# One decoder pass on one core: narrower masked products, a reordered triangular inverse, paired output-projection products, and the dense FFN's norm applied at gating

## Chip, cores and metric

One NeuronCore of a Trainium2 chip runs the whole kernel in one launch. The metric is the device time of the launch in microseconds (us); the profile's times count from the first instruction.

## What is computed

Two layers over 256 tokens of width 1024, all in float32. Each layer: `x = x + mixers(rms_norm(x) @ w_in) @ w_out`, then `x = x + ffn(rms_norm(x))`, where

```python
y = x * rsqrt(mean(x * x, axis=-1) + eps);  return y * w      # rms_norm
(silu(h @ w1) * (h @ w3)) @ w2                                # swiglu
```

The mixers are four groups of 256 columns: y_a (an RWKV-7 recurrence), y_b (dilated attention), y_c (MLA attention, whose latents c_q and c_kv are normalised first) and y_d (HGRN2, a gated linear recurrence). Layer 0 has a dense FFN of 2816 hidden columns; layer 1 routes each token to 2 of 8 experts of 3584 hidden columns. A last rms_norm gives the output.

## The kernel before

Everything is kept feature-major: 128 partitions hold features, 256 tokens lie along the free dimension; `xT` holds x and `hT` the normed x (later the mixers' output `yT`) as 8 tiles of 128x256. A large product is made in three: weight and activation are each split in a rounded high part (ACT copies to `mh`/`oh`/`wh`, `xh`, `gh`) and a low part (DVE subtracts: `ml`/`ol`/`wl`, `xl`, `gl`), and TensorE adds high x high, high x low, low x high in PSUM. Products of the mixers' small matrices are plain float32, which TensorE does as two instructions each. The engines' programs are straight lists written by hand (`block.tensor`, `block.scalar`, `block.vector`, `block.gpsimd`, `block.sync`); each engine works through its own list in order, and semaphores tie them. `spin(b, n)` (line 463) issues n products whose result nobody reads.

**HGRN2 scores** (lines 1294 to 1306). Levels 0 to 7; for a level e the queries and keys are scaled on POOL (lines 1153 to 1180), PE makes 8 products of 64x128 by 64x128 per level, and DVE copies under a mask (`hgrn_mask`, line 1994) into `hs`. For e >= 1 the mask has ones only in the later half of each block of 2^e columns. The levels stand between the last column units of `w_in` (units 9 to 12).

**The triangular inverse** (lines 1504 to 1547). RWKV's chunk form needs the inverse of 8 triangular 128x128 matrices. It is built in levels l = 1 to 6. A level is: 16 products `mtd x xin` (PE), a copy to `pid` (ACT, line 1824), products giving `xin` and `xit` updates (PE), subtractions (DVE, lines 2116 to 2132). The two 64-row halves of a matrix are separate until level 6, which joins them. `beside(l, half)` (line 1486) puts attention work between: MLA queries (`mla_q`) in level 1, their rotary partner in 2 and 3, `mla_k` in 4, `mla_v`, `mla_kr` in 5, and dilated attention. The DVE part of that work is `side_step(l)` (line 2081): reciprocal of the HGRN norm in 1, rotary for queries in 2 and 3, y_d in 4, rotary key in 5. Before the levels, DVE normalises the MLA latents (lines 2071 to 2077), and `mla_q(0)` waits for them (`lat_ready`).

**Solve** (line 1566). With the inverse, four heads are solved per chunk: for each head one product over 64 rows (`xi0`) and one over 128 rows (`xit`), each 64 outputs wide.

**Output projection** (lines 665 to 696). `w_out` is four units of 256 columns; unit u is summed in bank 2 + u. Its eight row tiles are taken in two halves: part 0 is y_b and y_d (k = 2, 3, 6, 7), part 1 is y_a and y_c (k = 0, 1, 4, 5). `pe_out_half(q)`, q = 0 to 7, makes 24 products of 256 columns. q = 0 to 3 stand amid the last attention work; q = 4 to 7 follow `attend_out(1)`, which turns y_c, and each waits for a weight half that is split into one of two buffers.

**After it** (lines 1633 to 1644, 1871 to 1888, 2198 to 2212). DVE adds bank 2 + u to `xT`, ACT squares, PE sums the squares (`norm_part`), ACT takes the root, DVE the reciprocal and the eight products into `hT`. In layer 0 `hT` is then split into `xh`, `xl`, and only then the dense FFN can begin. On DVE the first weight split of the FFN (`up(0, 0)`) stands before the last addition to `xT`:

```python
                    if u == NO - 1:
                        up(0, 0)
                    dve.wait_ge(sem("out_used"), 2 * NO * layer + NO + u + 1)
                    tt_(flat(xT[:, 2 * u:2 * u + 2]), ..., bank[2 + u][:], ALU.add, "xT_ready")
```

**The dense FFN** (lines 440 to 461, 557 to 586). Eleven pairs of 2x128 hidden columns. For a pair, PE does `up` in two parts (48 products each, banks 0, 1 or 6, 7 in turn) and `down` of the pair before it (48 products into banks 2 to 5, cleared at first by `zero_acc`). ACT takes silu of one half of a bank, DVE multiplies with the other (`dve_gate`, line 542), ACT and DVE split the result. Weights come as 1 MB stages through a ring of 7 slots that SyncE fills; slots 4 to 6 may be filled once `out_used` says that the first q of part 1 is done (lines 1054 to 1063). The MoE FFN has the same structure with jobs of 128 tokens; it starts with routing in layer 1.

## Time and profile before

| | us |
|---|---|
| median of 3 runs | 1687.99 (1687.73 to 1689.75) |
| the profiled execution | 1691.8 |
| its span, first to last instruction | 1690.2 |
| mean granted TensorE clock | 0.983 |
| mixers of layer 0, about | 0 to 230 |
| its projection's end, norm, dense FFN | 230 to 454 |
| mixers of layer 1, about | 454 to 670 |
| its projection's end, norm, routing | 670 to 715 |
| MoE FFN and the end | 715 to 1690 |

How to read it: PE is TensorE's matmuls, PEld its weight loads, DVE VectorE, ACT ScalarE, POOL GpSimd. The chain of waits is followed back from the last instruction, so a stretch of it says what set the time there. A PEclk of 1.00 is 2.4 GHz, 0.50 is 1.2 GHz; values between are means over a stretch that has both.

### The profile page before, as it was taken

What the parts mean: (1) busy time and instruction counts of PE and PEld (TensorE: products, weight loads), DVE (VectorE), ACT (ScalarE), POOL (GpSimd) and SP (SyncE); (2) the same over time, 40 slices, a digit from 0 to 9 for tenths busy, and PEclk for the clock granted to TensorE, in tenths of its full rate; (3) what the DMA queues carried; (4) which work ended last, traced back from release to release, by engine and by line L of the source; (5) the groups of instructions that cost most, each with busy time, mean ns of one, the idle gap of its engine ahead of it and who ended that gap; (6) DMA issues with size and microseconds to landing.
All of it is one profiled execution on the core that took longest, in us unless ns stands there. A gap on an engine that the chain in (4) does not pass through costs nothing.

```text
span 1690.2 us, 27508 instructions
## 1 busy us (share of the span) xinstructions
PE 1606.6 (95%) x10176; PEld 1368.0 (81%) x10176; DVE 1305.3 (77%) x1212; ACT 1041.2 (62%) x1032; POOL 133.6 (8%) x150
## 2 busy tenths in 40 slices
PE   7988989999898898899999999999999999999997
PEld 7876779999897777778888888888888888888776
DVE  4886555454557774688898888888889888888997
ACT  4634354433444344477777777777777777777675
POOL 1151000000003310100000000000000000000620
PEclk9998999999999999999999999999999999999999
DMA  7429044543242200789999999999999999999993
GB/s 249 163 80 405 31 174 179 193 175 124 75 156 91 76 2 7 297 319 373 363 397 368 369 395 373 379 383 373 382 375 363 396 368 373 391 373 366 396 355 119
DMA packets 68269, 457.51 MB, mean 271 GB/s; under 512 B 7296, under 2 KB 8480, under 8 KB 16752
## 3 DMA queue, kind: packets, MB, share of 16 engines
q1 hardware_dynamic: 59984, 425.80, 65.7%
q0 software_dynamic: 8080, 30.84, 4.7%
q8 instruction: 40, 0.66, 0.2%
q14 instruction: 21, 0.17, 0.0%
q10 hardware_dynamic: 144, 0.05, 0.0%
HBM read 433.07 MB, written 23.59 MB: 270 GB/s over the span
## 4 chain that ended last, share of the span: by engine, by line
PE 78%; DVE 11%; issue 5%; ACT 5%; DMA 0%; DVEq 0%; SPq 0%; ACTq 0%
PE bank L402 32%; PE bank L427 16%; PE bank L405 8%; PE bank L1203 7%; PE bank L660 6%; PE bank L431 4%; DVE wl L482 2%; ACT wh L478 1%; PE bank L415 1%; PE bank L692 1%; DVE ml L647 1%; DVE hT L1920 1%; PE bank L1551 1%; ACT mh L641 1%; ACT wide L1660 1%
## 5 line engine op out<-in xcount | busy, mean ns | idle before, releaser
L482 DVE TENSOR_TENSOR wl<-ring,wh 128x2048 fp32r<-128x2048 f32 x369 | 854.7, 2319 | 179.2 <-ACT wh L478 176.0
L478 ACT ACTIVATE wh<-ring 128x2048 fp32r<-128x2048 f32 x369 | 705.6, 1914 | 119.2 <-PE bank L427 47.7
L402 PE MATMUL bank<-wh,xh 128*128 128x512 f32 x896 | 359.6, 401 | 5.0 <-DVE wl L482 3.1
L402 PE MATMUL bank<-wh,xl 128*128 128x512 f32 x896 | 350.6, 391 | 0.0
L402 PE MATMUL bank<-wl,xh 128*128 128x512 f32 x896 | 349.2, 390 | 0.0
L402 PEld LDWEIGHTS bank<-wh,xh 128*128 128x128 f32 x896 | 168.2, 188 | 38.3 <-DVE wl L482 4.0
L402 PEld LDWEIGHTS bank<-wh,xl 128*128 128x128 f32 x896 | 168.1, 188 | 37.1
L402 PEld LDWEIGHTS bank<-wl,xh 128*128 128x128 f32 x896 | 168.7, 188 | 32.4
L427 PE MATMUL bank<-wh,gh 128*128 128x512 f32 x448 | 175.4, 392 | 6.4 <-DVE gl L555 6.4
L427 PE MATMUL bank<-wl,gh 128*128 128x512 f32 x448 | 174.4, 389 | 0.0
L427 PE MATMUL bank<-wh,gl 128*128 128x512 f32 x448 | 174.4, 389 | 0.0
L504 ACT ACTIVATE silu<-bank,const 128x256 f32<-128x256 f32 x134 | 62.3, 473 | 113.4 <-PE bank L402 72.4
L641 ACT ACTIVATE mh<-ring 128x1024 fp32r<-128x1024 f32 (+1 forms) x52 | 53.0, 1025 | 101.5 <-PE bank L660 101.2
L660 PE MATMUL bank<-xh,mh 128*128 128x256 f32 x336 | 99.9, 297 | 14.0 <-DVE xl L611 7.2
L517 ACT ACTIVATE gh<-bank 128x256 fp32r<-128x256 f32 x112 | 42.9, 383 | 112.7 <-PE bank L415 112.7
L647 DVE TENSOR_TENSOR ml<-ring,mh 128x1024 fp32r<-128x1024 f32 (+1 forms) x52 | 62.2, 1204 | 56.2 <-ACT mh L641 55.5
L427 PEld LDWEIGHTS bank<-wh,gh 128*128 128x128 f32 x448 | 84.1, 188 | 26.3 <-DVE gl L555 6.3
L405 PE MATMUL bank<-xh,wh 128*128 128x256 f32 x352 | 101.0, 287 | 3.4 <-DVE xl L611 3.4
L405 PE MATMUL bank<-xh,wl 128*128 128x256 f32 x352 | 100.7, 286 | 0.0
L405 PE MATMUL bank<-xl,wh 128*128 128x256 f32 x352 | 100.7, 286 | 0.0
L427 PEld LDWEIGHTS bank<-wh,gl 128*128 128x128 f32 x448 | 84.1, 188 | 17.6
L427 PEld LDWEIGHTS bank<-wl,gh 128*128 128x128 f32 x448 | 84.1, 188 | 17.1
(329 smaller groups left out, 2461.7 us busy)
## 6 DMA issues: line engine op xcount, KB each, us to landing
ring<-in_moe_w SPq DMA_DIRECT2D x336, 1024.0 KB, 6.3
ring<-in_ffn_w SPq DMA_DIRECT2D x33, 1024.0 KB, 4.8
ring<-in_w_in SPq DMA_DIRECT2D x24, 1024.0 KB, 5.0
ring<-in_w_out SPq DMA_DIRECT2D x8, 1024.0 KB, 4.8
job_x<-xrow POOLq DMA_DIRECT2D x1, 8192.0 KB, 27.4
job_y<-xrow POOLq DMA_DIRECT2D x1, 8192.0 KB, 46.8
xrow<-job_x POOLq DMA_DIRECT2D x7, 512.0 KB, 9.8
job_y<-yj POOLq DMA_DIRECT2D x7, 512.0 KB, 6.2
```

The lines of the kernel that those rows point to most:

```text
L402: ins = nc.tensor.matmul(up_bank(run, par, 0)[:], x[:, 0:C], w[b][:, k], **kw)
L405: ins = nc.tensor.matmul(up_bank(run, par, item)[:, kind * T:(kind + 1) * T], w[b][:, k, at:at + P], x, **kw)
L427: ins = nc.tensor.matmul(bank[2 + o][:], g[:, a, 0:C], w[b][:, a, o * 512:(o + 1) * 512], start=first and a == 0 and g is gh and b == 0, s ...
L431: ins = nc.tensor.matmul(bank[2 + o // 2][:, o % 2 * T:(o % 2 + 1) * T], w[b][:, a, o * P:(o + 1) * P], g[:, a], start=False, stop=False, ...
L478: nc.scalar.activation(wh[:, buf], flat_slot(slot), ACT.Copy).then_inc(sem("w_high"), 1)
L482: nc.vector.tensor_tensor(wl[:, buf], flat_slot(run.place(i)[0]), wh[:, buf].bitcast(F32), ALU.subtract).then_inc(sem("w_split"), 1)
L504: nc.scalar.activation(silu[:, item], up_bank(run, par, item)[:, 0:T], ACT.Silu, bias=cst("zero")).then_inc(sem("silu_done"), 1)
L517: nc.scalar.activation(o, i, ACT.Copy).then_inc(sem("g_high"), 1)
L641: nc.scalar.activation(mh[:, part, :, 0:n], unit_weights(u)[:, 4 * part:4 * part + 4, 0:n], ACT.Copy).then_inc(sem("unit_high"), 1)
L647: nc.vector.tensor_tensor(ml[:, part, :, 0:n], unit_weights(u)[:, 4 * part:4 * part + 4, 0:n], mh[:, part, :, 0:n].bitcast(F32), ALU.subtr ...
L660: ins = nc.tensor.matmul(o[:, c * T:(c + 1) * T], l, r, start=part == c == k == n == 0, stop=part == 1 and k == 3 and n == 2, skip_group_c ...
L1203: ins = nc.tensor.matmul(o, l, r, start=start, stop=stop)
```

## The change

1. HGRN2 levels e >= 1: PE and DVE treat only the later half of each block (64 columns per head instead of 128).
2. The inverse is kept as full 128x128 matrices (`xft`; POOL clears one quarter), and the solve is two products over all 128 rows per head.
3. The MLA latents' normalisation goes from before the levels into level 1, behind its updates, and the MLA steps on PE, ACT and DVE go one level later (`mla_kr` goes ahead of `mla_v`, y_d to level 6).
4. Ahead of the solve, `r_tokens(0)` and `attend_scores(4)` no longer wait for the inverse, and two of three spins go.
5. Part 1 of the output projection is taken as four pairs of units: q = 4, 5 with y_a's rows (k = 0, 1), ahead of and behind `attend_out(1)`, q = 6, 7 with y_c's (k = 4, 5). The three spins behind `attend_out(1)` go. Splits and additions are reordered to match; `up(0, 0)` on DVE now stands behind all additions.
6. Layer 0 only: `xh`, `xl` are the split of x times the norm's weight. The FFN's first products start on them; squares and sum are made meanwhile. The factor per token (`rstd[:, 1]`) comes at gating: DVE multiplies both halves of each bank by it (`dve_scale`), silu then works on that. `zero_acc` is replaced by start flags and a first step outside the loop.

The diff, cut to its core:

```diff
+        xft = proj[:, 4:8].rearrange("p a (b c) -> p (a b) c", c=P)
...
-            with pe.Fori(0, n // 2) as i:
-                step(2 * i + 1, 1)
+            step(1, 1, True)
+            with pe.Fori(0, (n - 1) // 2) as i:
                 step(2 * i + 2, 0)
-            if n % 2:
-                step(n, 1)
+                step(2 * i + 3, 1)
+            if n % 2 == 0:
+                step(n, 0)
...
+        def dve_scale(dve, run, m, par):
+            for item in range(run.parts):
+                dve.wait_ge(sem("stage_used"), run.up(m, 1)[0] + 1)
+                wait(dve, "g_split", run.before_pairs + m)
+                b = up_bank(run, par, item)
+                nc.vector.tensor_tensor(silu[:, item], b[:, 0:T], rstd[:, 1], ALU.mult)
+                nc.vector.tensor_tensor(gate[:, item], b[:, T:2 * T], rstd[:, 1], ALU.mult).then_inc(sem("scaled"), 1)
...
             for m in range(1, run.pairs - 1):
                 dve_gated_low(dve, run, m - 1)
                 up(m + 1, 0)
+                if not run.moe:
+                    dve_scale(dve, run, m, m % 2)
+                    up(m + 1, 1)
                 dve_gate(dve, run, m, m % 2)
-                up(m + 1, 1)
+                if run.moe:
+                    up(m + 1, 1)
                 down(m)
...
-        def pe_ffn_dense(pe):
-            zero_acc((2, 3, 4, 5))
-            for part in range(2):
-                pe.wait_ge(sem("x_split"), x_before(0, 2) + part + 1)
-                pe_up(pe, dense, 0, 0, part)
+        def pe_ffn_dense(pe, norm):
+            pe.wait_ge(sem("x_split"), x_before(0, 2) + 1)
+            pe_up(pe, dense, 0, 0, 0)
+            norm(1)
+            pe.wait_ge(sem("x_split"), x_before(0, 2) + 2)
+            pe_up(pe, dense, 0, 0, 1)
+            pe.wait_ge(sem("std_ready"), 2)
             pe_steps(pe, dense)
...
+                settle(nc.gpsimd.memset(xft[H:P, :, 0:H], 0.0))
...
-                            mm(bank[6 + half][:, m * P:(m + 1) * P], src, qry, sig=...)
+                                o = bank[6 + half][:, m * P // 2:(m + 1) * P // 2]
+                                qry = later(hq[lo:hi, (e - 1) % 2, s], e)
+                            mm(o, src, qry, sig=...)
...
-                    if (l, half) in ((1, 0), (1, 1)):
+                    if l == 2:
                         mla_q(half)
-                    if (l, half) in ((2, 1), (3, 0)):
-                        mla_partner(l - 2)
-                    if (l, half) in ((4, 0), (4, 1)):
+                    if (l, half) in ((3, 1), (4, 0)):
+                        mla_partner(l - 3)
+                    if l == 5:
                         mla_k(half)
                     if (l, half) == (5, 0):
+                        mla_kr()
+                    if (l, half) == (6, 0):
                         mla_v()
-                    if (l, half) == (5, 1):
-                        mla_kr()
...
-                        mm(o[0:H], xi0[0:H, m], rsol[0:H, h])
-                        mm(o[H:P], xit[:, m], rsol[:, h], sig=...)
+                        for q in (0, H):
+                            mm(bank[6][q:q + H, h * HD:(h + 1) * HD], xft[:, mat(h, c), q:q + H], rsol[:, h], sig=...)
...
+                r_tokens(0)
+                attend_scores(4)
                 spin(4, 1)
                 pe.wait_ge(sem("xit_ready"), nth(2 * LEVELS, 2 * LEVELS - 1))
-                r_tokens(0)
-                attend_scores(4)
-                spin(4, 2)
                 solve(0)
...
                 spin(6, 3)
+                pe.wait_ge(sem("ya_low"), nth(1))
+                pe_out_pair(pe, layer, NO, False)
                 attend_out(1)
-                spin(6, 3)
-                for u in range(NO):
-                    pe_out_half(pe, layer, NO + u)
-                    if u:
-                        norm_part(2 * layer + 1, u - 1)
+                pe_out_pair(pe, layer, NO + 1, False)
+                pe.wait_ge(sem("x_split"), x_before(layer, 1) + 2)
+                pe_out_pair(pe, layer, NO + 2, True)
+                if layer == 0:
+                    pe_out_pair(pe, layer, NO + 3, True)
+                    pe_ffn_dense(pe, norm)
+                    continue
+                pe_out_pair(pe, layer, NO + 3, True, lambda u: norm_part(2 * layer + 1, u - 2))
+                spin(6, 2)
+                norm_part(2 * layer + 1, 2)
+                spin(6, 1)
+                norm_part(2 * layer + 1, 3)
                 spin(6, 4)
-                norm_part(2 * layer + 1, NO - 1)
-                spin(6, (6, 4)[layer])
...
+                act_out_split(act, layer, NO + 2)
+                act_out_split(act, layer, NO + 3)
+                root_table()
+                if layer == 0:
+                    for half in range(2):
+                        for k in range(4 * half, 4 * half + 4):
+                            act.wait_ge(sem("xT_ready"), NO if half else k // 2 + 1)
+                            ins = nc.scalar.activation(xh[:, k], xT[:, k], ACT.Copy, scale=prm("ffn_norm", 0, k))
+                        ins.then_inc(sem("x_high"), 1)
+                        if half == 0:
+                            up(0, 0)
+                    for q in range(NO):
+                        square(n, q)
+                    up(0, 1)
+                    up(1, 0)
+                    root(n)
+                    act_ffn_dense(act)
+                    continue
...
-                dve_out_split(dve, layer, 4)
                 rwkv_out(3)
                 rwkv_out(4)
+                dve_out_split(dve, layer, 4)
+                out_low(0, yT[:, 0:2], "y_high", nth(2, 1), "ya_low")
                 normalise(1)
                 dve_out_split(dve, layer, 5)
-                out_low(0, yT[:, 0:2], "y_high", nth(2, 1))
                 out_low(2, turned1, "x_high", x_before(layer, 1) + 2, "x_split")
...
+                    if layer == 0 and u == 1:
+                        weighted_low(0)
+                up(0, 0)
+                if layer == 0:
+                    weighted_low(1)
+                    up(0, 1)
+                    up(1, 0)
+                    dve.wait_ge(sem("std_ready"), 2)
+                    recip(rstd[:, 1], rstd[:, 0])
+                    dve_ffn_dense(dve, tt_)
+                    continue
```

## Rows read from the trace of the kernel before

**Rows 1.** The page: the chain that ended last, by engine.

```profile
PE 78%; DVE 11%; issue 5%; ACT 5%; DMA 0%; DVEq 0%; SPq 0%; ACTq 0%
```

**Rows 2.** Stretches: length, busy PE, PEld, DVE, ACT, POOL, clock, DMA share, GB/s.

```profile
300.00:400.00 100.00, 100.00 (x835) 100.00 (x834) 47.32 (x35) 40.97 (x36) 0.00 (x0) 1.00 0.52 182
...
840.00:960.00 120.00, 119.79 (x544) 98.45 (x543) 107.27 (x73) 91.97 (x76) 1.07 (x2) 1.00 0.98 377
```

**Rows 3.** Groups by form, DVE and ACT, 0 to 460 us: busy us, mean ns, idle before.

```profile
L2003 DVE COPY_PREDICATED hs<-const,bank 128x512 f32<-128x512 int32 x14 | 10.3, 738 | 1.8 <-PE bank L1203 1.5
...
L546 DVE TENSOR_TENSOR gate<-bank,silu 128x256 f32<-128x256 f32 x22 | 8.8, 425 | 22.3 <-ACT silu L504 22.3
...
L504 ACT ACTIVATE silu<-bank,const 128x256 f32<-128x256 f32 x22 | 9.2, 470 | 41.0 <-PE bank L405 41.0
```

**Rows 4.** Timeline of layer 0 (start us, us, engine, line, output, inputs, forms, count).

```profile
106.80 1.16 PE L1203 MATMUL bank<-hq,hk 64*128 64x128 f32 x16
...
182.76 0.62 PE L1203 MATMUL bank<-proj,pts 128*64 128x64 f32 x12
...
190.81 2.12 PE L1203 MATMUL bank<-rsol,proj 64*64 64x64 f32 x16
...
196.47 0.66 PE L1551 MATMUL bank<-st,kap 64*128 64x64 f32 x8
```

**Rows 5.** The same, PE in the inverse of layer 1.

```profile
586.36 1.15 PE L1203 MATMUL bank<-proj,mtm 64*64 64x64 f32 x32 [0.22 <-DVE proj L2069]
...
591.73 3.41 PE L1203 MATMUL bank<-proj,wuq 128*96 128x256 f32 x8 [3.03 <-issue]
...
597.00 1.97 PE L1203 MATMUL bank<-proj,wuq 128*96 128x256 f32 x8
598.90 1.15 PE L1203 MATMUL bank<-proj,mtm 64*64 64x64 f32 x32
...
630.75 2.12 PE L1203 MATMUL bank<-rsol,proj 64*64 64x64 f32 x16
```

**Rows 6.** The same, DVE in that stretch.

```profile
586.71 3.35 DVE L1906 RECIPROCAL rstd<-rstd 128x512 f32<-128x512 f32 x1
```

**Rows 7.** Stretches of layer 0 with granted clock (the column of 0.50 and 1.00).

```profile
148.50:151.00 2.50, 2.47 (x6) 1.78 (x7) 0.81 (x2) 0.00 (x0) 0.00 (x0) 0.50 1.02 419
...
154.00:156.00 2.00, 2.00 (x33) 1.88 (x32) 1.78 (x5) 0.00 (x0) 0.00 (x0) 0.50 1.02 418
...
258.00:262.00 4.00, 3.98 (x18) 3.98 (x19) 4.00 (x3) 1.73 (x1) 0.00 (x0) 0.50 0.02 4
```

**Rows 8.** Chain of waits in order of time, 0 to 740 us (start, us, what).

```profile
223.29 1.22 DVE ol L681
...
230.60 4.14 PE bank L692 x24
...
244.27 1.93 ACT wh L478
246.29 2.29 DVE wl L482
...
253.58 3.26 DVE hT L1920 x8
...
258.02 25.74 PE bank L405 x192
...
301.05 5.76 PE bank L431 x48
...
663.22 1.22 DVE ol L681
...
692.46 3.25 DVE hT L1920 x8
```

**Rows 9.** Timeline, DVE in the dense FFN.

```profile
293.72 0.68 DVE L555 TENSOR_TENSOR gl<-gate,gh 128x512 fp32r<-128x512 f32 x1
```

**Rows 10.** Timeline, SyncE's queue: the FFN's weight loads.

```profile
234.76 36.36 SPq L1043 DMA_DIRECT2D ring<-in_ffn_w  x11
```

More of the change, by code:

```diff
@@ L445, in step @@
                 pe_up(pe, run, m, par, 1)
[L446 removed]
+                if first and run.moe:
                     wait(pe, "acc_copied", 2 * j)
@@ new lines, in out_source @@
+        def out_source(q):
+            if q < NO:
+                return out_half(ring[:, (NU + q) % RING_M], 0), (q,)
+            k = 4 * (q // NO - 1) + 4 * ((q - NO) // 2)
+            if q % 2 == 0:
+                return ring[:, 1:3, k:k + 2], (0, 1)
+            return ring[:, 0:4:3, k:k + 2], (3, 2)
+        def act_out_split(act, layer, q):
+            src, units = out_source(q)
+            for u in units:
+                slot = (NU + u) % RING_M
+                act.wait_ge(sem(f"w_ready{slot}"), 16 * (before(2 * layer, slot) + (NU + u) // RING_M + 1))
+            wait(act, "out_used", OUTS * layer + q - 1)
+            nc.scalar.activation(oh[:, q % 2].rearrange("p (a c) t -> p a c t", a=2), src, ACT.Copy
```

157 lines of the change are left out of this document (87 added, 70 removed).

## The prediction

> **What bounds the kernel now.** I read the chain by engine first: PE holds 78% of it [rows 1]. The stretches then tell two kinds of time apart. In the dense FFN and in the MoE FFN PE is busy throughout at full clock [rows 2]; nothing that the change does there makes a product less, so those stretches keep their length, and what starts them earlier ends the kernel earlier. DMA's share of 0.98 in the MoE stretch leaves little room, but its loads also start earlier (they wait for the output projection). The second kind is the mixers and the norm behind them, where the chain jumps between PE, DVE and ACT [rows 8]. The gain must come from there, in two layers. I walk each piece on the profile's clock, first as if nothing before it had moved.
>
> **HGRN2 levels.** A masked copy of 128x512 is 0.738 us; of 256 columns I take 0.425, the row of a DVE operation on 128x256 from PSUM [rows 3]. Fourteen a layer become shorter, but only four stand on the chain: the two of level 1, ahead of the split of unit 10, and the two of level 6, ahead of level 7's products. Four times 0.31 is 1.25 us. PE: 16 instructions with 128 columns moving took 1.16 us. With 64 columns moving and the same 64x128 weights, eight took 0.66, so each further one about 0.055, and 16 would take about 1.1 [rows 4]. Four such groups on the chain give 0.25. Sum 1.5 a layer, **3.0**; bounds 0.5 (strided copies that cost what full ones did) and 5. The Trainium skill (TensorE: Matmul & The Clock Gate, Back-to-back issue gap) gives columns over 2.4 GHz plus 2.5 ns as the gap of isolated matmuls, with a floor near 25 ns; by it a group would lose some 0.4 us, and the sum here would be about 5.3. It also says that the weight load shares in the pace of a real stream, which is how I read the row.
>
> **The inverse and the MLA steps.** Before, in layer 1, the reciprocal of the latents' norms starts at 586.71; PE stands 3.03 us for it, until 591.73, and then runs `mla_q(0)` in 3.41 where the same eight took 1.97 later [rows 5, 6]. After, DVE first waits 2 us for PE's products, then does four updates (1.8) and a score block (1.3). The reciprocal starts at about 591.9 and the latents are ready at 596.8, 5.2 later. PE meanwhile does the rest of level 1 and the start of level 2 (some 4.1) and then stands at `mla_q(0)` again, for 3.8. So the stall isn't removed, it moves to level 2, and PE is 1.1 behind when it resumes; I take the half clock behind it as unchanged. DVE's level 5 now carries two long items (rotary part, two weight splits, rotary key), so `kf_ready` comes 0.5 late for `mla_v` in level 6. Two spins fewer ahead of the solve give 0.9 back. POOL's clearing of a quarter of `xft` is one operation of 512 elements, ahead of POOL's wait for DVE: idle time, cost 0. Solve(0) starts 0.6 to 0.7 later.
>
> The solve itself: 16 instructions that alternate 64 and 128 rows took 2.12 us; twelve of one shape, 128 rows by 64 outputs, took 0.62 [rows 4]. That is about 0.036 each, so 16 take 0.8: 1.3 less, twice a layer, both on the chain. Net 2.6 - 0.6 = 2.0 a layer, **4.0**. Bounds: the solve gives nothing (-1.3) to no stall at all (+12).
>
> **Output projection, both layers.** In layer 0's clock: DVE's split for q = 4 at 223.29 [rows 8] stands, before, ahead of six operations that give y_a. After, these start at 221.6 and y_a is ready at 224.3; ACT, busy with q = 5 until 224.9, gives its high part at 225.6, DVE the low part at 226.3. PE does 24 products (2.9: 48 took 5.76 [rows 8]) until 229.3, turns y_c, does 24 more until 232.6. Queued behind these on ACT and DVE: the y_c split (until 231.3), the splits of q = 6 (until 233.0; its buffer is free at 229.3) and q = 7. PE does q = 6 from 233.05 and q = 7 until 238.8. Before, q = 4 began at 230.60 and q = 7 ended at 242.6: 3.8 earlier.
>
> **Layer 1 behind it.** DVE adds until 240.7. Before, its weight split (2.29, ending at 248.6, behind ACT's 1.93) stood ahead of the last addition [rows 8]; now it stands behind. PE does the four sums with three spins until 244.3; root 0.5, reciprocal 1.75, and the eight products of 3.25 end at 249.9. Before they ended at 695.71, which is 255.8 in this clock (663.22 answers to 223.29 [rows 8]). Gain **5.9**.
>
> **Layer 0 behind it.** ACT takes weighted high parts of 128x256 at 0.47, the row of its silu [rows 3]: half 0 ready at 237.9, then 1.93 for the stage's high part (239.8). DVE: low parts (4 x 0.41, the rate of the eight in 3.26) until 239.6, two additions until 240.9, the stage's low part until 243.2. There the FFN starts; it used to at 258.02 [rows 8]. The stage is loaded: the queue's first weight load, issued at 234.76 [rows 10], now goes at 229.4. PE has stood for 4.4 us, so it starts at half clock, as it did before [rows 7]: 192 products took 25.74 where four times 5.76 is 23.04, so 2.7 lost [rows 8]. First 48 until 251.7; then the norm's sums, 4.1, which now stand between; ACT's squares end long before. The next 48 end at 261.6 and pair 1's 96 at 273.1, against 283.76 before. Gain **10.7**. The root waits for the sums, `std_ready` comes at 256.3, the factor at 258, before the first scaling at 261.6.
>
> **The scaling in the loop.** Four more DVE operations of 0.425 a pair, 1.7 us, and the silu behind them; DVE's split of `up(m+1, 1)` now also stands ahead of the gate. Cover: in pair 1 the gated values were split at 294.4 and PE wanted them at 301.05, 6.65 us of slack [rows 8, 9]. Cost 0. If the slack were gone, each us would cost 10 us. `zero_acc` and the loop's unrolled steps: 0, within 0.5 either way.
>
> **Sum.** 3.0 + 4.0 + 5.9 + 10.7 = 23.6 us. Against the profiled execution's 1691.8 that gives 1668.2; the median of the runs lies 3.8 below it, and the same step from 1687.99 gives 1664.4.
>
> **Rivals.**
> A. *The clock holds at the moved stall.* Before, layer 0 ran 8.3 us at 1.2 GHz behind it (three stretches of 0.50, 148.5 to 156, the first and last shown [rows 7], and a little more), which costs about 4.1, and layer 1 about 1.4 [rows 5]. PE is now busier just before the stall. For: the clock changes with what came before. Against: the wait is longer, 3.8 against 3.03. Gain 5.5 more: 1659.
> B. *The clock falls where spins went.* The Trainium skill (the same page, What's actually happening) makes the gate halve the clock of an idle engine, which speaks against taking spins out. Here: 24 products took 4.14 instead of 2.9 at 230.60 after such an idle stretch, 1.2 lost, and 2.7 at 258.02 [rows 8]. If q = 4 and q = 6 in both layers fall, some 1.2 to 2.7 each, that costs about 8: 1672.
> C. *The deferral brings nothing of its own.* If stage weights or ACT's queue hold the first products, layer 0 gains there only what layer 1 does, 5.9 instead of 10.7: 1669.
> D. *Slower: the gate becomes the bound.* Place: `down` of each of ten pairs waits for `g_split`. It decides once the added path exceeds the slack of 6.65; to undo 23.6 and lose 3.5 more it needs 2.7 beyond it per pair: 9.4 us added where I count some 4, half of that beside ACT's work. Time then 1691. Against: DVE is busy for only 47 of 100 us there [rows 2].
>
> **Chances.** Forecast 0.58, own range 1660 to 1669 (HGRN and solve bounds, a few us of clock); A 0.14; B 0.17; C 0.08; D 0.03. The range to 8 in 10 takes in A's and B's centres or nearly: 1657 to 1674. A measurement of this kernel tells about 0.2% (3.4 us) from no change; only D, or a failure of several pieces at once, comes there: faster 0.96, same 0.02, slower 0.02.
>
> **What would show it.** Right: masked copies near 0.43; solves near 0.8; the first `up` product near 239.7 (243.2 less the 3.5 of the two first pieces) and at half clock; `hT` in layer 1 some 23 earlier than 695.7; MoE stretches of unchanged pace. Wrong: masked copies still 0.74; PE standing in level 2 for much more or less than 3.8; PE waiting for `gl` in the dense loop; granted clock of 0.5 in the output projection; a first FFN product that waits for a weight load.

## The result and the profile after

The changed kernel took **1665.73 us** in the median of four runs (1662.51 to 1671.7), beside 1688.28 for the kernel before on the same chip: a ratio of 0.9876, 95% interval 0.9861 to 0.989. Forecast were 1664.4 and 1657 to 1674. Its profiled execution is the fastest of the four, 1662.51 with a span of 1660.9; the prediction put a profiled execution at 1668.2.

I cut both spans at the same instructions. "Last reduction" is the start of the 256-column reduction of the last score block; gains are before less after.

| from, to | layer 0, us | layer 1, us | gain, both | forecast |
|---|---|---|---|---|
| span's start to the first product | 21.47, 22.39 | | -0.9 | 0 |
| first product to level 1 of the inverse | 121.69, 120.26 | 123.50, 118.15 | 6.8 | 3.0 |
| level 1 to solve(0) | 47.65, 45.08 | 44.39, 48.15 | -1.2 | -1.3 |
| solve(0) to the last reduction | 29.64, 26.77 | 29.63, 26.78 | 5.7 | 5.2 |
| last reduction to the end of pair 1's up products | 63.32, 50.92 | | 12.4 | 10.7 |
| from there to layer 1's first product | 179.09, 179.10 | | 0.0 | 0 |
| last reduction to the end of `hT` | | 35.33, 28.68 | 6.7 | 5.9 |
| from there to the span's end | | 994.5, 994.6 | -0.1 | 0 |

The sum is 29.3, the difference of the two spans; the medians differ by 22.6. The count x8 or x16 of a row is of instructions, two for each plain float32 product. The second row of the table is mostly a matter of the clock: layer 1's first 192 products took 25.84 before and 23.31 here, and the eight kernels below that start layer 1 in the same way take 120.1 to 122.0 for this stretch. The rest of the text is about which gains belong to the change.

The inverse, after: the timeline of PE in both layers (`mla_q(0)`, then the solve), which answers to [rows 4, 5]; and of DVE, which answers to [rows 6].

```profile
153.24 3.34 PE L1264 MATMUL bank<-proj,wuq 128*96 128x256 f32 x8 [3.74 <-issue]
...
187.73 0.69 PE L1264 MATMUL bank<-rsol,proj 128*64 128x64 f32 x16
...
573.27 3.70 PE L1264 MATMUL bank<-proj,wuq 128*96 128x256 f32 x8 [3.75 <-issue]
580.38 3.12 PE L1264 MATMUL bank<-proj,wuq 128*96 128x256 f32 x8
...
610.82 0.69 PE L1264 MATMUL bank<-rsol,proj 128*64 128x64 f32 x16
```

```profile
568.25 3.35 DVE L1985 RECIPROCAL rstd<-rstd 128x512 f32<-128x512 f32 x1
571.64 1.53 DVE L1982 SCALAR_TENSOR_TENSOR proj<-proj,par,rstd 128x256 f32<-128x256 f32 x3
```

The bracket is PE's idle time: the stall has moved to level 2 and grown from 3.03 to 3.75. The word "issue" in it names no cause; DVE's rows give it, since the latents are ready at 573.2. The solve fell from 2.12 to 0.69. Behind the stall layer 1 pays at half clock, as the stretches show (the column of 0.50 and 0.81), which answer to [rows 7]:

```profile
573.30:582.00 8.70, 8.70 (x48) 5.95 (x49) 3.83 (x8) 0.58 (x1) 0.00 (x0) 0.50 0.00 0
582.00:584.00 2.00, 2.00 (x16) 1.37 (x17) 2.00 (x1) 0.40 (x1) 0.00 (x0) 0.81 0.00 0
```

The chain of waits through the output projection and the FFN's start in layer 0, which answers to [rows 8]:

```profile
220.30 3.11 PE bank L731 x24
...
226.83 3.10 PE bank L731 x24
...
234.80 2.30 DVE wl L488
237.10 0.14 issue
237.24 7.47 PE bank L413 x48
244.70 3.45 PE bank L1264 x16
248.16 17.27 PE bank L413 x144
```

Both groups of 24 run at full clock (3.1, where 4.14 was paid before). What the FFN waits for is DVE's low part of the weights, not the norm any more. The first 48 products take 7.47, 1.7 more than the 5.76 of full clock; the norm's sums stand between, 3.45; and 144 products then take 17.27, three times 5.76, so the added scaling delays nothing. Between the projection's last product, which ends at 232.8, and the FFN's first, PE stands for 4.5 us. The MoE stretch is untouched, as against [rows 2]:

```profile
820.00:940.00 120.00, 119.79 (x544) 98.56 (x543) 107.29 (x73) 91.93 (x76) 1.07 (x2) 1.00 0.97 378
```

### The profile page after: what moved, and what is told of

It is laid out like the page before. It is cut to its first block, busy times and chain, and to the rows that moved or that the text cites. A ratio compares the mean times of both kernels' runs of the same rounds, so it can differ in the third digit from the quotient of the medians.

```text
span 1660.9 us, 27440 instructions
## 1 busy us (share of the span) xinstructions
PE 1583.0 (95%) x10130; PEld 1353.2 (81%) x10130; DVE 1309.5 (79%) x1254; ACT 1043.9 (63%) x1038; POOL 135.0 (8%) x152
## 4 chain that ended last, share of the span: by engine, by line
PE 78%; DVE 11%; issue 6%; ACT 4%; DMA 0%; DVEq 0%; SPq 0%; ACTq 0%
PE bank L410 33%; PE bank L435 17%; PE bank L413 8%; PE bank L1264 6%; PE bank L695 5%; PE bank L439 4%; DVE wl L488 2%; PE bank L731 1%; PE bank L423 1%; DVE ml L682 1%; ACT wh L484 1%; PE bank L1269 1%; PE bank L1616 1%; DVE rw L1976 1%; DVE rw L1979 1%
## 5 line engine op out<-in xcount | busy, mean ns | idle before, releaser
L515 ACT ACTIVATE silu<-bank,const 128x256 f32<-128x256 f32 x112 | 53.0, 473 | 72.1 <-PE bank L410 72.1
```

Of the source, the lines that this page charges most:

```text
L515: nc.scalar.activation(silu[:, item], up_bank(run, par, item)[:, 0:T], ACT.Silu, bias=cst("zero")).then_inc(sem("silu_done"), 1)
```

## Experiments

### Is the moved stall worth anything, and what does it cost?

**The MLA steps back.** The changed kernel with the latents and the MLA steps at their old levels.

```diff
-                    if l == 2:
+                    if (l, half) in ((1, 0), (1, 1)):
                         mla_q(half)
...
-                def latents():
-                    dve.wait_ge(sem("latstd_ready"), nth(2, 1))
+                dve.wait_ge(sem("latstd_ready"), nth(2, 1))
```

> The changed kernel with the MLA steps and the latents' norm where they stood before (the latents ahead of the levels, mla_q in level 1); the rest of the change stays. Read: the stretch from the first product of level 1 to solve(0), which took 45.1 us in layer 0 and 48.2 in layer 1 of the changed kernel, and 47.7 and 44.4 before. Theory (the stall is only moved; what differs is the clock behind it): the stretch is what it was before less the two spins' 0.9, that is 42.7 at full clock plus half of the time that the trace shows at half clock, so 46.8 in layer 0 if the clock falls as before and 43.5 in layer 1; at equal clock within 1 us of the changed kernel. Rival (the move itself relieves DVE's level 1 and is worth about 2 us a layer): with the lost clock taken off, this kernel is still 1.5 us or more a layer behind. PE's idle ahead of mla_q(0) is 3.0 in both. Total within 4 us of the changed kernel either way by the theory, 4 or more above it by the rival.

Measured: 1662.97 us (1659.34 to 1665.93), ratio 0.9851 [0.9831, 0.9871]. From level 1 to solve(0): 44.54 and 43.97 us. Its timeline of PE in layer 1, and the stretches behind:

```profile
574.42 3.55 PE L1264 MATMUL bank<-proj,wuq 128*96 128x256 f32 x8 [3.02 <-issue]
```

```profile
574.42:576.50 2.08, 2.08 (x6) 1.37 (x7) 0.77 (x2) 0.00 (x0) 0.00 (x0) 0.54 0.00 0
576.50:578.50 2.00, 2.00 (x8) 1.09 (x6) 0.00 (x0) 0.44 (x1) 0.00 (x0) 0.63 0.00 0
```

A granted clock of 0.54 over 2.08 us and of 0.63 over 2.00 us loses 1.7 us (the same in layer 0, with 0.56 over 1.90 and 0.57 over 2.00). If all of that is paid, the stretch without it is 42.3 us in layer 1 and 42.8 in layer 0.

**Spins in the stall.** The changed kernel with PE kept at work while it waits.

```diff
                         pe.wait_ge(sem("hoss_used"), nth(1))
+                        spin(0, 7)
                         pe.wait_ge(sem("lat_ready"), nth(3, 2))
```

> The changed kernel with seven spins (products of 256 columns into bank 0, which is free) in mla_q(0), between its first and its second wait, so that PE is idle for about 0.5 us instead of 3.7 while DVE takes the latents' reciprocal. Nothing else changes; the products start at the same time. Theory (PE's idle time is what lets the clock fall): granted clock 1.00 behind the stall in both layers, the stretch from level 1 to solve(0) takes 43.3 to 44.0 in both, instead of 45.1 and 48.2; total about 1.5 to 6 us less. Rival (the clock there follows something else, such as small products with few rows): 0.5 to 0.8 is still granted behind the stall in at least one layer and the stretch stays within 0.7 us of 45.1 or 48.2. Third (spins delay the products that follow): mla_q(0) starts later by 0.3 or more after lat_ready.

Measured: 1661.24 us (1658.32 to 1664.22), ratio 0.9845 [0.9827, 0.9863]. The stretch took 44.27 and 43.66 (the theory had 43.3 to 44.0). Layer 1's timeline, and the stretch that holds the spins and the one behind:

```profile
578.20 1.97 PE L1264 MATMUL bank<-proj,wuq 128*96 128x256 f32 x8 [0.48 <-DVE proj L1983]
```

```profile
572.00:578.20 6.20, 5.22 (x77) 4.33 (x73) 5.96 (x8) 3.12 (x7) 1.46 (x2) 1.00 0.01 3
578.20:580.00 1.80, 1.80 (x8) 1.22 (x8) 0.82 (x2) 0.00 (x0) 0.00 (x0) 1.00 0.00 0
```

The eight instructions of `mla_q(0)` take 1.97 instead of 3.70, at a granted clock of 1.00, and start no later than before, 10.6 us behind the start of level 1. So idle PE is what let the clock fall, and it cost the changed kernel's profile 0.8 us in layer 0 (45.08 less 44.27) and 4.5 in layer 1 (48.15 less 43.66). It also gives the price of the move at full clock, this kernel less the one with the steps back: 44.3 - 42.8 and 43.7 - 42.3, **1.4 us a layer**. The move loses that and gives nothing, so the theory of the experiment before (the stall is only moved) holds and its rival falls; its bound of 1 us between the two kernels at equal clock was too narrow. The median of the kernel with the steps back is 2.8 below the changed one's first median, with ranges that overlap.

**Two reciprocals.** The changed kernel with the query latents' factor first; `mla_q(0)` waits for these alone.

```diff
-                    recip(flat(rstd[:]), flat(rstd[:]))
+                    recip(rstd[:, 0], rstd[:, 0])
                     for k in range(2):
...
+                    recip(rstd[:, 1], rstd[:, 1])
...
-                        pe.wait_ge(sem("lat_ready"), nth(3, 2))
+                        pe.wait_ge(sem("lat_ready"), nth(3, 1))
```

> The changed kernel with the latents' reciprocal of 128x512 (3.35 us) cut in two of 256 columns: that of the query latents first, with its two products, and mla_q(0) waits for these alone; that of the key and value latents behind them, waited for at mla_k(0). Theory (mla_q(0) waits for the reciprocal and for nothing else): PE's idle ahead of mla_q(0) falls from 3.7 to about 1.6 (1.7 of reciprocal and 0.5 of the third product less), DVE is done at the same time as now or 0.1 later, while PE does mla_q(0); the stretch from level 1 to solve(0) is about 2.1 us shorter a layer at equal clock, and the clock loses less; total 4 to 8 us less. Rival (DVE's queue is what paces the levels, and the stall turns up again): PE waits as much longer for xin or xit of level 2, the stretch is within 0.5 us of 45.1 and 48.2 once the clock is taken off.

The wait for the other half, ahead of `mla_k(0)`, is left out of the lines above. Measured: **1655.42 us** (1654.52 to 1657.57), ratio 0.9814 [0.9798, 0.9831]. The stretch took 41.77 and 41.55, 2.5 and 2.1 below the kernel with spins. In the timeline and the stretches of layer 1:

```profile
571.52 1.94 PE L1264 MATMUL bank<-proj,wuq 128*96 128x256 f32 x8 [1.62 <-issue]
```

```profile
569.90:571.50 1.60, 0.00 (x0) 0.01 (x1) 1.49 (x4) 1.56 (x4) 0.00 (x0) 1.00 0.00 0
571.50:573.50 2.00, 1.98 (x9) 1.32 (x10) 1.96 (x2) 0.35 (x2) 0.00 (x0) 1.00 0.00 0
```

The wait is for the reciprocal alone, and DVE has room for its second half while PE is at `mla_q(0)`. After 1.6 us of idle time here the clock stayed at 1.00; after 3.0 in the kernel with the steps back and 3.7 in the changed one it did not.

### What is the deferral worth?

**No deferral.** The changed kernel with the norm ahead of the dense FFN again, as in layer 1; the loop has no scaling.

```diff
-                if layer == 0:
-                    pe_out_pair(pe, layer, NO + 3, True)
-                    pe_ffn_dense(pe, norm)
-                    continue
                 pe_out_pair(pe, layer, NO + 3, True, lambda u: norm_part(2 * layer + 1, u - 2))
...
                 spin(6, 4)
+                if layer == 0:
+                    pe_ffn_dense(pe)
```

> The changed kernel without its deferral in layer 0: the norm's sums, root, reciprocal and eight products stand ahead of the split of x and of the dense FFN, as in layer 1, and the loop has no scaling. The new order of the output projection, the solve, the levels and the MLA steps stay. Read: from the end of the last score reduction of RWKV/MLA ahead of the output to the end of pair 1's up products: 50.9 us in the changed kernel, 63.3 before. Theory (the deferral is worth its own 4.8 us, as in the sum: 10.7 against 5.9): 55.7, with an uncertainty of 1.5 for the clock at the start of the FFN; total about 4.8 above the changed kernel. Rival C (the stage's weights hold the first products anyway): 51 to 52, total within 1. Third (the deferral is worth more, because the norm's sums now hide behind the weight split): 58 or more. If the scaling in the loop costs anything, pairs would take less than 17.3 us each here; by the theory they do not.

Measured: 1672.41 us (1669.07 to 1675.11), ratio 0.9916 [0.9896, 0.9936]. Its chain from the norm on:

```profile
238.53 1.76 DVE rstd L1942
240.29 0.02 issue
240.32 3.26 DVE hT L1956 x8
243.57 1.15 DVE xl L616
244.72 0.04 issue
244.76 25.04 PE bank L413 x192
```

The last reduction started at 214.89, so pair 1's products end 54.9 us behind it (269.80 less 214.89), not 50.9: the deferral is worth **4.0 us** (4.8 forecast), or 3.7 with each profile's loss of clock at these products taken off (2.0 here, 1.7 with it). The first product is 7.1 later than with it, and the 3.45 of the sums no longer stand in the way. Rival C falls. The median is 6.7 above the changed kernel's first and 4.5 above its second. The other 8.4 of layer 0's 12.4 come with the new order of the projection, its splits and its additions: 7.7 until the end of `hT` (36.39 behind the reduction before, 28.69 here), of which the clock at q = 4 is 1.0, and 0.7 because the first 192 products took 25.04 and not 25.74. Pairs take 17.28 here as there, so the scaling costs nothing.

**Spins ahead of the dense FFN.** The changed kernel with one line more.

```diff
                     pe_out_pair(pe, layer, NO + 3, True)
+                    spin(6, 12)
                     pe_ffn_dense(pe, norm)
```

> The changed kernel with twelve spins (bank 6) in layer 0 between the last product of the output projection and the first of the dense FFN, where PE stands for 7.3 us. Theory (the idle time lets the clock fall, and the first products are paid at 1.2 GHz): granted clock 1.00 at the first 48 products, which take 5.8 to 6.1 us instead of 7.47; from the last score reduction to the end of pair 1's up products 49.2 to 49.6 us instead of 50.9; total 1.5 less. The spins take 0.24 each, 2.8 together, so PE still stands for about 4.4 ahead of the first product; second theory (only idle time just ahead counts): then the clock still falls and the 48 take 7.0 or more, as after 5 us of idle without the deferral. Third (spins take room in PE's queue and delay the start): first product later than 22.9 us behind the reduction.

Measured: 1671.32 us (1662.37 to 1673.85), ratio 0.9909 [0.9891, 0.9927]; the profiled run is its fastest. Its chain:

```profile
227.33 5.93 PE bank L731 x48
233.26 5.18 PE bank L476 x24
238.44 5.74 PE bank L413 x48
```

A spin takes 0.43 and not 0.24 (x24 is 12 spins), and PE stands there for 4.5 us and not for the 7.3 of the expectation, which are counted from the end of q = 6. So 5.18 us of spins end 0.7 too late: the first product comes 23.45 behind the reduction (214.99) instead of 22.74, as the third theory has it. Still the clock holds, the 48 products take 5.74, and pair 1 ends 49.92 behind it, 1.0 better than 50.92. The first theory is right on the clock, but its stretch of 49.2 to 49.6 and its total were missed. The second falls. The median is 5.6 above the changed kernel's first and 3.4 above its second; the ranges overlap, so neither a loss nor a gain in the total is shown. The runs at 1669.65 and more have a clock of 0.981 to 0.983, the profiled one 0.990; I have no profile of a run where this kernel lost it, so where it was lost isn't known.

### The parts of the mixers

**The solve's shape alone**, in the kernel before.

```diff
-                        o, m = bank[6][:, h * HD:(h + 1) * HD], mat(h, c)
-                        mm(o[0:H], xi0[0:H, m], rsol[0:H, h])
-                        mm(o[H:P], xit[:, m], rsol[:, h], sig="u_ready" if h == NH - 1 else None)
+                        for q in (0, H):
+                            mm(bank[6][q:q + H, h * HD:(h + 1) * HD], xft[:, mat(h, c), q:q + H], rsol[:, h],
+                               sig="u_ready" if h == NH - 1 and q else None)
```

> The kernel before with one part of the change alone: the inverse's last two levels are written to one tile whose rows and columns are both 128 deep, one quarter cleared by POOL, so that the solve's 16 products all have 128 rows and 64 outputs instead of alternating 64 and 128 rows; one spin ahead of solve(0) instead of three. Theory (mixing the two shapes is what made 16 products take 2.12 us): each solve 0.7 us, solve(0) to the last score reduction 26.8 us instead of 29.6 in both layers; with the spins, solve(0) starts 0.9 us earlier behind level 1, clock aside; total 6 to 8 us below the kernel before. Rival (the 2.8 us a layer come from the new order around it, such as the MLA steps at other levels, not from the shape): solves of 0.7 but solve(0) to the last score reduction still 28 us or more.

Measured in one run: 1684.18 us. Solves of 0.69, the timeline of PE:

```profile
190.49 0.69 PE L1205 MATMUL bank<-rsol,proj 128*64 128x64 f32 x16
196.74 0.69 PE L1205 MATMUL bank<-rsol,proj 128*64 128x64 f32 x16
```

Solve(0) to the last reduction takes 26.77 in both layers instead of 29.64 and 29.63: the whole of that row's gain is the shape. The stretch ahead of it is 0.97 and 0.93 shorter, about the two spins' 0.9. The rival falls. Nor are 64 rows slow by themselves: 32 instructions of that form alone took 1.15 [rows 5]. The median of the runs beside it is only 2.3 higher, not these 7.6; but its mean clock is 0.983, theirs 0.986 to 0.990. Beside the profiled execution of the kernel before, which also had 0.983, its span is 7.6 shorter (1690.2, 1682.6), though the clock fell at partly other places in the two.

**The weight split behind the last addition alone**, in the kernel before.

```diff
                 for u in range(NO):
-                    if u == NO - 1:
-                        up(0, 0)
                     dve.wait_ge(sem("out_used"), 2 * NO * layer + NO + u + 1)
                     tt_(flat(xT[:, 2 * u:2 * u + 2]), flat(xT[:, 2 * u:2 * u + 2]), bank[2 + u][:], ALU.add, "xT_ready")
+                up(0, 0)
```

> The kernel before with one edit: DVE's low split of the next FFN's first stage (2.29 us, which waits for ACT's 1.9) stands behind the last of the four additions to xT instead of ahead of it. Theory: in layer 1 the last addition starts when q = 7's products end, 684.4 instead of 687.4 on the profile's clock, and square, sums and root follow 3.0 earlier; from the last score reduction to the end of hT 32.3 us instead of 35.3, and 3 less in layer 0 too; so 3.0 of the 6.7 us gained there belong to this one line, and 3.7 to the new order of the products. Rival (the split is only put in front of the reciprocal then, and the chain gets it back): 34.5 us or more. Total about 6 us less, or under 2.

Measured in one run: 1688.7 us. The stretch to the end of `hT` is 34.02 us in layer 1, 1.3 less, and not 3.0: it lies between the theory and the rival. In layer 0 it is 34.02 too, 2.4 less, of which 1.0 is the clock at q = 4. The last addition is 2.0 earlier behind the reduction (25.0 instead of 27.0). The chain shows what took part of it back:

```profile
682.91 0.86 PE bank L1203 x4
683.78 1.73 PE bank L466 x8
685.50 0.88 PE bank L1203 x4
```

Four spins (L466), hidden before under DVE's split, now stand in front of the last of the norm's sums. The total shows no gain beside runs of a higher clock (0.986 to 0.990, here 0.983): solve(0) to the last reduction, which this edit doesn't touch, took 31.16 in layer 0 where it was 29.64, since the clock fell at 199.8. The profiled execution of the kernel before, at 0.983, is 3.1 longer.

**The same line undone in layer 1 of the changed kernel.**

```diff
                 for u in range(NO):
+                    if layer and u == NO - 1:
+                        up(0, 0)
```

> The changed kernel with one part undone in layer 1 alone: DVE's low split for the next FFN's first stage stands ahead of the last addition again. In the changed kernel the last addition starts at 656.85, ACT's high part is there at 658.0. Theory: the addition ends at 661.0 instead of 657.5, the square at 661.8, sums and root 2.3 later than now; from the last score reduction to the end of hT 31.0 us instead of 28.7. So this line is worth more in the new order, where the products are done early, than in the old one, where it gave 1.3. Rival (its worth is the same in both orders): 30.0.

Measured: the stretch is 31.06 us, 2.4 more, as the theory has it (31.0), and not 30.0; 1666.5 us in one run. DVE's timeline:

```profile
658.70 2.29 DVE L488 TENSOR_TENSOR wl<-ring,wh 128x2048 fp32r<-128x2048 f32 x1 [2.87 <-ACT wh L484]
660.91 0.68 DVE L1976 TENSOR_TENSOR xT<-xT,bank 128x512 f32<-128x512 f32 x1
...
664.20 1.75 DVE L1985 RECIPROCAL rstd<-rstd 128x256 f32<-128x256 f32 x1 [2.61 <-ACT rstd L1729]
```

DVE stands 2.87 for ACT's high part with the addition queued behind, and the products are done. So of layer 1's 6.7 us some 2.4 hang on this line, given the new order of the products (which also has fewer spins), and 1.3 with the old one.

**The masked copies.** They take, in the timeline of the changed kernel's layer 0, 0.75 each in levels 1 and 2 and 0.45 from level 3 on, half of the rows below. The experiment gives levels 1 and 2 other patterns in target and mask; its scores are therefore wrong, and only its times are read.

```profile
95.54 1.52 DVE L2083 COPY_PREDICATED hs<-const,bank 128x256 f32<-128x256 int32 x2
104.03 1.51 DVE L2083 COPY_PREDICATED hs<-const,bank 128x256 f32<-128x256 int32 x2
109.61 0.90 DVE L2083 COPY_PREDICATED hs<-const,bank 128x256 f32<-128x256 int32 x2
```

```diff
+                            if e <= 2:
+                                near = [x[:, :, 0:H].rearrange("p a (b i) -> p a b i", i=run_) for x in (o, over(lvl(e - 1), 4))]
+                                if layer == 0:
+                                    to = near[0]
+                                if (layer == 0) == (e == 1):
+                                    mask = near[1]
```

> The changed kernel with other access patterns in its masked copies of levels 1 and 2, so that parts of the HGRN2 scores go to wrong columns or are masked by the wrong ones; the amount of elements is the same. These copies take 0.75 us each with runs of one element (level 1) and two (level 2), 0.45 with runs of four or more. Layer 0, level 1: target and mask both in 64 consecutive columns. Layer 0, level 2: target consecutive, mask in runs of two. Layer 1, level 1: unchanged. Layer 1, level 2: target in runs of two, mask consecutive. Theory (the short run in the mask's read of SBUF costs): 0.45, 0.75, 0.75, 0.45. Rival (the short run in the write costs): 0.45, 0.45, 0.75, 0.75. Third (both, or neither: two-column halves cost by themselves): 0.45, 0.75, 0.75, 0.75, or 0.75 throughout. Total unchanged within 2 us.

Measured, two copies a row (layer 0's levels 1 and 2, then layer 1's):

```profile
95.73 0.94 DVE L2091 COPY_PREDICATED hs<-const,bank 128x256 f32<-128x256 int32 x2
104.28 0.92 DVE L2091 COPY_PREDICATED hs<-const,bank 128x256 f32<-128x256 int32 x2
...
521.61 1.51 DVE L2091 COPY_PREDICATED hs<-const,bank 128x256 f32<-128x256 int32 x2
530.10 1.50 DVE L2091 COPY_PREDICATED hs<-const,bank 128x256 f32<-128x256 int32 x2
```

That is 0.46, 0.46, 0.75, 0.75: the rival. A mask read in runs of two costs nothing, and a target written in runs of two costs as much as the full copy did (0.74). For runs of one, target and mask changed together, so which of them costs isn't separated. The theory falls. The total, 1666.67 us in one run, is within the changed kernel's range.

### The clock, and the best version

**The changed kernel again**, with no edit.

> The changed kernel itself, as it is, once more beside the other kernels of this call, since its first four runs lie 9 us apart. If the spread is that of the clock, time and mean granted clock go together here (some 1.7 us for 0.001) and the median is 1663 to 1670. Its stretches by the profile: solve(0) to the last score reduction 26.8 in both layers, from there to the end of hT 28.7, to pair 1's end 50.9 within 1.5; a clock that falls adds to the stretch in which it falls and to no other.

Measured: 1667.93 us (1662.16 to 1669.09), ratio 0.9873 [0.9853, 0.9892]; the stretches 26.78, 26.78 and 28.66, and 51.4 to pair 1's end (266.46 less 215.05; the first 48 products took 7.94). Its runs are 1667.79, 1669.09, 1668.08 and 1662.16 at mean clocks of 0.984, 0.985, 0.984 and 0.989. With the first four (1662.51, 1671.7, 1667.3, 1664.16 at 0.988, 0.982, 0.986, 0.987) that is about 1.4 us for each 0.001: time and clock go together, as expected (1.7). The kernel before spread less, 1685.89 to 1690.21 in the nine runs beside.

**Two reciprocals and spins.** The kernel with two reciprocals and the spins named in the expectation.

```diff
                 norm(2 * layer)
-                spin(6, 8)
+                spin(6, 15)
...
                 if u == 9 and 0 in parts:
-                    spin(b, 6)
+                    spin(b, 10)
...
                         pe.wait_ge(sem("hoss_used"), nth(1))
+                        spin(0, 2)
...
                     pe_out_pair(pe, layer, NO + 3, True)
+                    spin(6, 9)
                     pe_ffn_dense(pe, norm)
...
                 norm_part(2 * layer + 1, 3)
-                spin(6, 4)
+                spin(6, 6)
```

> The changed kernel with the two reciprocals of the run before, and spins in five places where PE stands and the clock fell behind it in the profiles: 15 instead of 8 ahead of each layer's first product, 10 instead of 6 ahead of unit 9, two ahead of mla_q(0), nine ahead of the dense FFN, six instead of four ahead of the router. A spin takes 0.43 us (24 rows in 5.18), not the 0.24 that I wrote for the run with twelve. Theory (what is left of the time at half clock follows idle PE): the profile's stretches below full clock ahead of the MoE, which summed to about 12 us lost in the two-reciprocal kernel's profile at places that change from run to run, shrink to 4 or less; time 1647 to 1651, and its runs lie within 4 us of each other. Rival (spins that delay a product cost what they give back, or the clock falls elsewhere for it): 1653 or more. As the twelve spins' median of 1671 was above the changed kernel's although its profile was not, a third: spins make the clock fall more often in runs that are not profiled; then 1658 or more.

Measured: **1650.88 us** (1649.18 to 1653.45), ratio 0.9781 [0.9768, 0.9794], mean clocks of 0.992 to 0.995. Its chain in layer 0:

```profile
230.63 2.30 DVE wl L488
232.94 0.14 issue
233.07 5.99 PE bank L413 x48
```

It is 2.2% below the kernel before and 1% below the changed one, and its runs lie 4.3 us apart. Three short falls of the clock are left ahead of the MoE (about 1.7 us each, near 102, 485 and 665), 5 us instead of the theory's 4 or less, and the spread of 4.3 is just above its 4; its time came. The third theory falls: with nine spins ahead of the FFN, no higher median showed. Which of the five places gave how much of the 4.5 between the medians isn't separated.

**The HGRN2 part undone in that kernel**: products and copies over all 128 columns.

```diff
-                                o = bank[6 + half][:, m * P // 2:(m + 1) * P // 2]
-                                qry = later(hq[lo:hi, (e - 1) % 2, s], e)
...
-                            settle(nc.vector.copy_predicated(later(o, e), later(over(lvl(e - 1), 4), e).bitcast(I32), i),
-                                   "hgrn_masked")
+                            settle(nc.vector.copy_predicated(o, over(lvl(e - 1), 4).bitcast(I32), i), "hgrn_masked")
```

> The kernel with two reciprocals and spins, whose clock is the steadiest, with the HGRN2 part of the change undone: products and masked copies of levels 1 to 7 take all 128 columns again. Read: layer 1 from its first product to level 1 of the inverse, 119.67 us with the change. In its chain stand the copies of levels 1 and 2 (0.75 each, which are as long when full), the two of level 3 (0.44 against 0.74 when full) and four groups of 16 products (1.04 against some 1.15). Theory: 0.6 and 0.4, so 120.7 us, a gain of 1.0 a layer and 2.0 in all, 1653 us. Rival (the sum of my prediction, 1.5 a layer): 121.2 and 1654. Second rival (the copies are not on the chain at all): 119.7 to 120.1. A granted clock under 1.00 in the stretch is taken off before comparing.

Measured: 1651.73 us (1650.42 to 1653.27), ratio 0.9791 [0.9766, 0.9816]. First product to level 1: 120.45 in layer 0 (119.44 with the part), 119.54 in layer 1 (119.67). In layer 0 both reach the first masked copy 71.6 us behind the first product, and both have one stretch of 3.4 us at 0.50 around the second pair of copies, so 1.0 is the part's gain there. In layer 1 the clock fell ahead of the levels with the part (at 483.9) and within them without it (at 519.4), so this pair alone can't be read.

Other kernels' profiles fill that gap. From the first masked copy to level 1, where the clock fell some 12 us behind the first products of the levels, three kernels with the part took 47.81 to 47.85 us (layer 1 of those without deferral, with twelve spins and with the steps back), and those without it 48.45 to 48.48 (the kernel before and this one in layer 1, the one with the split behind in both layers). That is 0.6 a layer. Two of these, the kernel with twelve spins and then this one (47.81 and 48.48 between the starts of the two rows):

```profile
516.30 1.51 DVE L2084 COPY_PREDICATED hs<-const,bank 128x256 f32<-128x256 int32 x2
564.11 1.15 PE L1264 MATMUL bank<-proj,mtm 64*64 64x64 f32 x32 [0.22 <-DVE proj L2151]
```

```profile
510.78 1.51 DVE L2082 COPY_PREDICATED hs<-const,bank 128x512 f32<-128x512 int32 x2
559.26 1.15 PE L1264 MATMUL bank<-proj,mtm 64*64 64x64 f32 x32 [0.22 <-DVE proj L2148]
```

So the part gives 0.6 to 1.0 a layer, 1.3 to 2.0 in both; the second rival (nothing) falls, and so does the prediction's 1.5 a layer. The theory's 1.0 set a start-to-start time of a group (1.04) against a duration (1.15); like against like the halved columns save 0.05 a group (1.16 to 1.11), so its sum is 0.8. The medians say 0.9 for both layers, with ranges that overlap, and the ratios to the kernel before beside them 1.7.

## Why the prediction was right

The forecast case came: a median 1.3 us from 1664.4 (3.5 in the second set), faster by about 1.2%. The mechanisms of its two large terms were right; that the total came so close is partly luck, as the sum below shows. Term by term:

- **HGRN2 levels, forecast 3.0, found 1.3 to 2.0.** The failed step is the price of 0.425 for each of the fourteen masked copies of 256 columns: those of levels 1 and 2 stayed at 0.75. Two of the four that I put on the chain were level 1's. The PE groups went from 1.16 to 1.11: of the two prices that the prediction gives for a group, 0.06 and 0.4 us, the first came (by the second its sum would be 5.7, not the 5.3 written there). The table's 6.8 is not this part's; most of it is clock.
- **Inverse, MLA steps and solve, forecast 4.0, found about 4.8.** The stall moved to level 2 at 3.75 us (3.8 forecast). The move costs 1.4 a layer with the spins' gain kept apart, where 0.6 to 0.7 with 0.9 of spins taken off makes 1.5. The two solves and what follows gave 2.9 a layer instead of 2.6, since 16 instructions took 0.69 and not 0.8. So twice 2.9 + 0.9 - 1.4, at equal clock.
- **"I take the half clock behind it as unchanged"** was wrong in both layers, in opposite ways: layer 0 lost 0.8 to it where the prediction read 4.1 from the kernel before, layer 1 lost 4.5 instead of 1.4. The two nearly cancel in the profile. Rival A (the clock holds at the moved stall) is false: it fell in both layers, and only with PE kept at work, or with half the stall, did it hold.
- **Rival B** (the clock falls where spins went) is false: q = 4 and q = 6 took 3.11 and 3.10 at 1.00 in layer 0, and no fall stands at them in layer 1 either. PE has q = 5 to do between the chain's two groups, so it is hardly idle there. The idle stretch that does cost is the one ahead of the FFN, as forecast. Idle PE did halve the clock in this case: with spins in the wait the same eight instructions took 1.97 us instead of 3.70. By the Trainium skill (TensorE: Matmul & The Clock Gate, What's actually happening) the clock gate halves the clock of an idle engine; the runs with spins agree.
- **Layer 1 behind the last reduction, forecast 5.9, found 6.7**, of which 2.4 hang on the order of one split and one addition.
- **Layer 0, forecast 10.7, found 12.4.** The walk through the queues was exact: first FFN product 22.75 behind the reduction forecast (243.2 less 220.45), 22.74 found. What was off are two sizes behind it, the clock's loss (1.7, not 2.7) and the norm's sums (3.45, not 4.1). The deferral's own share is 4.0, not 4.8, and the new order's 8.4, not 5.9. Of these 2.5 more, 1.8 is that without the deferral the FFN starts 29.9 behind the reduction and not 31.7 (1.0 of it is the clock at q = 4, which layer 0 lost before), and 0.7 the shorter fall at the FFN's first products.
- **Rivals C and D** are false: 4.0 us go when the deferral goes, and the loop's rhythm of 17.28 a pair is the same with and without scaling.

The terms sum to 25.2 to 25.9 (1.3 to 2.0, then 4.8, 6.7 and 12.4), beside 23.6 forecast and 22.6 and 19.8 in the medians of the two sets. Some 2 of layer 0's 12.4 are clock: q = 4 took 3.11 and not 4.14, and 1.7 and not 2.7 were lost at the FFN's start. So the levels were put 1.0 to 1.7 too high and the other three terms 3.3 too low, and the medians lie 3 to 6 us below what the stretches add up to. The clock can account for that, since the longer stall cost up to 4.5 in layer 1 and the changed kernel's runs spread over 10 us, but no run separates it. A spread of that size is also why a median 1.3 us from the forecast is partly luck.

## What to carry to other kernels

A stall that is moved is paid again, in waiting and in the clock behind it: ask which operation it waits for and split that one (here a reciprocal of which half was needed first, some 10 us between the medians), instead of placing the work one level later. Walk each queue where an order is changed, and look for the long operation that waits for another engine ahead of a short one that somebody needs. Judge a small change by stretches cut at fixed instructions: one profile may be the fastest of its kind, as here, where it showed 29 us for a change worth some 21.

## What the runs showed of the hardware

- Sixteen instructions that alternate between two shapes (64 and 128 rows) took 2.12 us, sixteen of 128 rows 0.69, though the second form multiplies more; 32 of 64 rows alone took 1.15.
- COPY_PREDICATED of 128x256 from PSUM: 0.45 us where the target is written in runs of four elements or more, and 0.75 with runs of one or two. A mask in runs of two cost nothing beside a target in runs of 64 (0.45); a mask in runs of one was never tried alone.
- Behind the stall at `mla_q(0)` the clock fell in every profile with 3.0 or 3.7 us of idle PE and held with 1.6 or 0.5. That is no rule: ahead of layer 1's first product PE stands for 3.33 us in the changed kernel and in the one with two reciprocals, and the clock held in the one profile (192 products in 23.31) and fell in the other. The same stall cost 0.8 us in layer 0 and 4.5 in layer 1, and from run to run the clock moved the changed kernel by up to 10 us.
